# Layer 0's first norm: GpSimd adds pairs of squared tiles, and four products with ones sum them in place of eight

## The chip, the cores and the metric

The kernel runs on one NeuronCore of one Trainium2 chip. A time is device microseconds (us) of one execution; lower is better. The engines are TensorE (PE; PEld is its weight load), VectorE (DVE), ScalarE (ACT), GpSimd (POOL) and SyncE (SP, which issues the DMAs). Each takes its own instructions in the order of the program, and they meet through semaphores only.

## What is computed

A decoder trunk of two layers, on 512 tokens of width 1024. Each layer takes an RMS norm, one input projection whose columns go to four token mixers (differential attention, a short gated convolution, a diagonal state-space model "S5", and Mamba-2), an output projection and a residual; then a second norm and a gated feed-forward part. The change touches only the first norm of layer 0:

```python
def rmsnorm(x, g):
    xf = x.astype(jnp.float32)
    y = xf * lax.rsqrt(jnp.mean(xf * xf, axis=-1, keepdims=True) + EPS)
    return (y * g.astype(jnp.float32)).astype(x.dtype)
...
    for l in range(DEPTH):
        h = rmsnorm(x, ln1_g[l])
        proj = h @ w_in[l]
```

## The kernel before

The activations lie transposed: `x` is 8 tiles (`KD`) of 128 channels by 512 tokens. All large products run as "units": one unit makes 128 output rows from 8 tiles. To keep float32 accuracy out of a faster matmul type, each operand is split in a high part and a low part (`xh` and `xl`, `wh` and `wl`), and a unit is three passes of 8 matmuls: `xl`·`wh` (L504), `xh`·`wh` (L506 or L509) and `xh`·`wl` (L517). For each unit SP loads `raw`, ACT copies it to `wh` (L903), and POOL forms `wl = raw - wh` (L362); buffers are double, so the load of a unit waits for the `wl` of the unit two before it, and the order on POOL (`low()` calls between other work for S5) is written out by hand.

The gain is folded into `xh` and `xl`, so the units of a norm can start before the norm's root is known; the factor `rbc` (one per token, the same in all partitions) multiplies the results as DVE takes them out of PSUM (`scaled`, L1201). In layer 0, for each tile `k`: ACT makes `xh` (L912) and the square of the tile in `G[:, k % 2]` (L918); DVE makes `xl` (L1187, inputs `x` and `xh` in SBUF); TensorE runs `first_square(k)`, a float32 product of a 128x128 block of ones with the square (L530), summing over the channels in bank 7, and then the two products of unit 0 with tile `k`. ACT's square of tile `k` waits for the product of tile `k - 2`, since `G` has two places for it. When the eighth is summed, ACT forms `rbc` (L924, L926).

Between the `xl` tiles DVE also runs the first steps of the S5 tables (`s5_phases`, L1329 to L1342), one step after each tile, then `s5_decay` (L1346 to L1354) and `s5_values` (L1361 to L1381), which waits for sines that ACT computes from the phases. Only then it takes out units 0 and 1 (L1201, tile `z`). POOL, after the `wl` of units 0, 1 and 2, waits for that first `z` (`unit_out`) before its S5 work begins (`power_terms`, L398), and the `wl` of unit 3 stands behind it.

Of the kernel before, what the change touches and what calls it, by code (L numbers as in the profile page):

```python
# [10 lines left out]
ALU = mybir.AluOpType  # L11
ACT = mybir.ActivationFunctionType
# [4 lines left out]
KD = D // P  # L17
# [55 lines left out]
def build(nc, A):  # L73
    with ExitStack() as ctx:
        arena_end = [0]

        def sb(name, shape, dt=F32, at=None):

            size = int(np.prod(shape[1:])) * (2 if dt == BF16 else 4)
            size = -(-size // 32) * 32  # L80
            off = arena_end[0] if at is None else at
            if at is None:
                arena_end[0] += size
            offsets[name] = off
            return nc.alloc_sbuf_tensor_at(name, list(shape), dt, offset=base + off)

        def sem(name):
            return ctx.enter_context(nc.semaphore(name))
# [6 lines left out]
        x = sb("x", [P, KD, T])  # L95
        xh = sb("xh", [P, KD, T], F32R)
        xl = sb("xl", [P, KD, T], F32R)
# [14 lines left out]
        G = sb("G", [P, 6, T])  # L112
# [21 lines left out]
        def early(name, shape, dt=F32):  # L134
            t = sb(name, shape, dt, at=pre_end[0])
            pre_end[0] += -(-int(np.prod(shape[1:])) * 4 // 32) * 32
            return t
# [6 lines left out]
        ones0 = early("ones_first", [P, P])  # L144
        phases = []
        for l in range(L):
# [35 lines left out]
        bank = [ctx.enter_context(nc.psum_tensor(f"bank{b}", [P, T], F32)) for b in range(8)]  # L182
# [9 lines left out]
        act_bank = [sem(f"act_bank{b}") for b in range(8)]  # L192
        dve_free = [sem(f"dve_free{b}") for b in range(8)]
        act_free = [sem(f"act_free{b}") for b in range(8)]
        unit_done, unit_out, resid = sem("unit_done"), sem("unit_out"), sem("resid")
# [3 lines left out]

        x_loaded = [sem(f"x_loaded{k}") for k in range(KD)]  # L200
        rates_loaded, lam_go, lam_exp, mask_ready = [sem(n) for n in ("rates_loaded", "lam_go", "lam_exp", "mask_ready")]
        ones_ready, sq_summed = sem("ones_ready"), sem("sq_summed")
        pre_loaded, par_loaded, cst_loaded, late_loaded = [
            sem(n) for n in ("pre_loaded", "par_loaded", "cst_loaded", "late_loaded")]
        mats_full, out_done = sem("mats_full"), sem("out_done")
# [5 lines left out]
        xh_full, sq_full, sq_free, xk_ready, rms_ready = [  # L211
            sem(n) for n in ("xh_full", "sq_full", "sq_free", "xk_ready", "rms_ready")]
# [31 lines left out]
        def counter():  # L244

            at = {}

            def nth(s, k=1):
                at[s.num] = at.get(s.num, 0) + k
                return at[s.num]  # L250
            return nth
# [16 lines left out]
        def par_of(l, name, i=0, n=1):  # L268
            return par_all[:, l, PARAMS[name][0] + i:PARAMS[name][0] + i + n]
# [79 lines left out]
        def _(pool):  # L349
            nth = counter()  # L350
            own, owned = chain(pool_own)
            tt = nc.gpsimd.tensor_tensor
            unit = iter(range(len(UNITS)))
            temp_free = []

            def low():
                g = next(unit)
                p, cols = g % 2, COLS[g]
                pool.wait_ge(wh_full, g + 1)
                if g >= 2:  # L360
                    pool.wait_ge(unit_done, g - 1)
                tt(wl[:, p, 0:cols], raw[:, p, 0:cols], wh[:, p, 0:cols].bitcast(F32),  # L362
                   ALU.subtract).then_inc(wl_full, 1)
# [75 lines left out]

            nc.gpsimd.memset(ones0[:, :], 1.0)  # L440
            nc.gpsimd.memset(eps_all[:, :], EPS).then_inc(ones_ready, 1)
            for l in range(L):
                low()
                for s in range(NIN - 1):
                    low()
                    if s == 1:
                        power_terms(l, 0)
                        nc.gpsimd.memset(kernels[:, :, :, :], 0.0)
                    if 2 <= s <= 4:
                        for n in ((1, 2), (3,), (4, 5))[s - 2]:  # L450
                            power_terms(l, n)
                    if s == 5:
                        pool.wait_ge(late_loaded, 32)
                        output_matrix(l)
                    if 6 <= s <= 8:
                        state_terms(l, s - 6)
                    if 9 <= s <= 10:
                        table(l, 0, s - 9)
                    if 11 <= s <= 12:
                        for n in ((3, 4), (5,))[s - 11]:  # L460
                            state_terms(l, n)
                    if 13 <= s <= 14:
                        table(l, 1, s - 13)
                    if 17 <= s <= 24 and s - 17 != WHOLE_MEAN:
                        pool.wait_ge(sqk_ready, 8 * l + s - 16)
                        tt(sq_low[:, :], G[:, 2, :], sq_high[:, :].bitcast(F32), ALU.subtract).then_inc(sqk_low, 1)
                    if s in (15, 21):
                        s5_imaginary(l, (s - 15) // 6)
                for _ in range(16 + 2 * (2 * FHALF + 8)):
                    low()  # L470
# [3 lines left out]
        def _(pe):  # L474
            mm = nc.tensor.matmul
            nth = counter()
# [4 lines left out]
            def claim(b, freed, k=1):  # L481

                if b in free_at:
                    pe.wait_ge(*free_at[b])
                if freed is xbc_silu:
                    raised(unit_out)
                free_at[b] = (freed, raised(freed, k))

            def unit(b, K, hi, lo, out, ready=None, within=None, each=None):

                g = next(number)
                p = g % 2
                assert b % 2 == p
                pe.wait_ge(wh_full, g + 1)
                claim(b, out)

                parts = [range(K)] if ready is None else [range(K - 1), [K - 1]]
                for part, ks in enumerate(parts):
                    for k in ks:
                        if ready is not None:  # L500
                            if each is not None:
                                each(k)
                            pe.wait_ge(ready, nth(ready))
                        mm(bank[b][:, :], wh[:, p, k * P:(k + 1) * P], lo[:, k, :], start=(k == 0), stop=False)  # L504
                        if ready is not None:
                            w = mm(bank[b][:, :], wh[:, p, k * P:(k + 1) * P], hi[:, k, :], start=False, stop=False)  # L506
                    if ready is None:
                        for k in ks:
                            w = mm(bank[b][:, :], wh[:, p, k * P:(k + 1) * P], hi[:, k, :], start=False, stop=False)  # L509
                    if ks[-1] == K - 1:  # L510
                        w.then_inc(wh_free, 1)
                    if within is not None:
                        within()
                    if part == 0:
                        pe.wait_ge(wl_full, g + 1)
                    for k in ks:
                        w = mm(bank[b][:, :], wl[:, p, k * P:(k + 1) * P], hi[:, k, :], start=False, stop=(k == K - 1))  # L517
                w.then_inc(unit_done, 1)
# [2 lines left out]
                for i in range(n):  # L521
                    unit(i % 2, K, hi, lo, out, ready if i == 0 else None)

            def first_square(k):

                if k == 0:
                    pe.wait_ge(ones_ready, 1)
                    claim(7, act_free[7])
                pe.wait_ge(sq_full, nth(sq_full))
                w = mm(bank[7][:, :], ones0[:, :], G[:, k % 2, :], start=(k == 0), stop=(k == KD - 1))  # L530
                w.then_inc(*((sq_summed, 1) if k < KD - 1 else (act_bank[7], 1)))

            def rms_sum():

# [241 lines left out]
            early_hi, early_lo = mh[:, MIXB:MIXED, :], ml[:, MIXB:MIXED, :]  # L776
            for l in range(L):
                if l == 0:
                    unit(0, KD, xh, xl, unit_out, xk_ready, each=first_square)
                else:  # L780
                    unit(0, KD, xh, xl, unit_out, xk_ready)
                    rms_sum()
# [103 lines left out]
        def _(act):  # L886
            fn = nc.scalar.activation
            nth = counter()
            unit = iter(range(len(UNITS)))
# [15 lines left out]
            def norm_tile(l, k, gain, arrived=None):  # L905

                n, p = next(normed), k % 2
                if arrived is None:
                    act.wait_ge(resid, nth(resid))
                else:  # L910
                    act.wait_ge(arrived[k], 16)
                fn(xh[:, k, :], x[:, k, :], ACT.Copy, scale=par_of(l, gain, k)).then_inc(xh_full, 1)  # L912
                if arrived is None:
                    if n - 1 > KD:
                        act.wait_ge(sq_free, n - 1 - KD)
                elif k >= 2:
                    act.wait_ge(sq_summed, k - 1)
                fn(G[:, p, :], x[:, k, :], ACT.Square).then_inc(sq_full, 1)  # L918

            logged = counter()  # L920

# [35 lines left out]
            for l in range(L):  # L957
# [143 lines left out]
                for n in range(STEPS):  # L1101
# [5 lines left out]
                    w = (n % NQ + 1) * P  # L1107
# [780 lines left out]
```

## Time and profile before

| | us |
|---|---|
| median of 3 timed runs | 1314.2 |
| lowest, highest | 1313.98, 1315.82 |
| span of the profiled execution | 1310.8 |
| PE busy in the span | 1290.9 |
| DVE busy | 849.4 |
| POOL busy | 637.2 |
| ACT busy | 493.5 |

The span goes from the first to the last instruction of the profiled execution. The page gives no time of that execution from outside; against the median of the timed runs the span is 3.4 us short, which is what lies around it. The granted clock of TensorE is 1.000 over the span. Busy time of PE is not time at its peak, since matmuls are pipelined and their ends are modelled.

### The profile page before, as it was taken

The page shows a single profiled execution, that of the slowest core. Times are in us where ns is not written, and L with a number is a line of the kernel's source. Part 1 is how long each engine was busy: PE and PEld are TensorE (multiplying, and loading weights), DVE is VectorE, ACT ScalarE, POOL GpSimd, SP SyncE. Part 2 cuts the span into 40 slices and gives each one's busy share as a digit, 9 for nine tenths or more (in the row PEclk, how much of TensorE's full clock was granted, in tenths as well). Part 3 has the DMA queues.
Part 4 walks back from the last instruction along what each step waited for, and adds up shares of the span by engine and source line. Part 5 has one row for each costly group of instructions (what it writes and reads, how often), then busy time and mean ns, then how long its engine had stood idle before and what let it go on. Part 6 is the DMA issues. An engine that isn't in the chain of part 4 may idle for free.

```text
span 1310.8 us, 15989 instructions
## 1 busy us (share of the span) xinstructions
PE 1290.9 (98%) x6218; PEld 1054.8 (80%) x6218; DVE 849.4 (65%) x1142; ACT 493.5 (38%) x758; POOL 637.2 (49%) x302
## 2 busy tenths in 40 slices
PE   7999999999999999999999999999999999999999
PEld 4888886787888888888878888867878888888887
DVE  8789885846888117775237799677477761377720
ACT  6332556744223112223344245566432221122220
POOL 2986661144444444444468776512444444444442
PEclk9999999999999999999999999999999999999999
DMA  6232331123333323333232322301333233233332
GB/s 222 81 97 65 97 89 33 28 94 113 97 97 115 101 74 97 97 98 110 84 111 82 87 65 92 87 25 53 99 106 97 97 106 103 81 97 97 109 111 87
DMA packets 40939, 120.49 MB, mean 92 GB/s; under 512 B 6432, under 2 KB 10656, under 8 KB 40864
## 3 DMA queue, kind: packets, MB, share of 16 engines
q1 hardware_dynamic: 40864, 119.46, 29.3%
q8 instruction: 50, 0.82, 0.3%
q14 instruction: 25, 0.20, 0.0%
HBM read 114.20 MB, written 2.10 MB: 89 GB/s over the span
## 4 chain that ended last, share of the span: by engine, by line
PE 90%; DVE 5%; ACT 2%; POOL 2%; DMA 1%; issue 1%; SPq 0%; POOLq 0%; ACTq 0%
PE bank L504 26%; PE bank L517 26%; PE bank L509 25%; PE bank L718 3%; PE bank L506 1%; ACT G L1079 1%; PE bank L766 1%; DMA raw<-in_w_in 1%; POOL wl L362 1%; PE bank L663 1%; PE bank L755 1%; DVE G L1568 1%; PE bank L596 1%; PE bank L611 1%; DVE ssum L1196 1%; PE bank L745 1%
## 5 line engine op out<-in xcount | busy, mean ns | idle before, releaser
L362 POOL TENSOR_TENSOR wl<-raw,wh 128x1024 fp32r<-128x1024 f32 (+3 forms) x208 | 507.1, 2439 | 629.4 <-ACT wh L903 385.1
L903 ACT ACTIVATE wh<-raw 128x1024 fp32r<-128x1024 f32 (+3 forms) x208 | 218.6, 1052 | 267.3 <-PE bank L509 207.9
L504 PE MATMUL bank<-xl,wh 128*128 128x512 f32 x1088 | 282.4, 397 | 0.0
L517 PE MATMUL bank<-xh,wl 128*128 128x512 f32 x1088 | 271.1, 391 | 0.0
L509 PE MATMUL bank<-xh,wh 128*128 128x512 f32 x1056 | 261.0, 389 | 0.0
L504 PEld LDWEIGHTS bank<-xl,wh 128*128 128x128 f32 x1088 | 202.8, 188 | 48.2 <-issue 5.9
L517 PEld LDWEIGHTS bank<-xh,wl 128*128 128x128 f32 x1088 | 203.2, 188 | 41.7
L509 PEld LDWEIGHTS bank<-xh,wh 128*128 128x128 f32 x1056 | 198.3, 188 | 41.5
L1230 DVE TENSOR_TENSOR x<-x,bank 128x512 f32<-128x512 f32 x64 | 43.9, 685 | 228.5 <-PE bank L517 228.4
L504 PE MATMUL bank<-ml,wh 128*128 128x512 f32 x512 | 137.5, 395 | 0.0
L517 PE MATMUL bank<-mh,wl 128*128 128x512 f32 x512 | 127.5, 389 | 0.0
L509 PE MATMUL bank<-mh,wh 128*128 128x512 f32 x456 | 112.9, 389 | 0.0
L517 PEld LDWEIGHTS bank<-mh,wl 128*128 128x128 f32 x512 | 96.1, 188 | 20.0
L504 PEld LDWEIGHTS bank<-ml,wh 128*128 128x128 f32 x512 | 95.3, 188 | 20.8 <-issue 1.4
L1145 ACT ACTIVATE G<-G 128x512 f32<-128x512 f32 x44 | 27.8, 632 | 208.9 <-DVE G L1213 208.9
L1589 DVE TENSOR_TENSOR G<-G 128x512 f32<-128x512 f32 x44 | 101.1, 2298 | 4.6
L509 PEld LDWEIGHTS bank<-mh,wh 128*128 128x128 f32 x456 | 85.6, 188 | 18.0
L1208 DVE TENSOR_SCALAR G<-pad,par_all 128x512 f32<-128x512 f32 x48 | 89.9, 1873 | 1.5
L1201 DVE TENSOR_TENSOR G<-bank,rbc 128x512 f32<-128x512 f32 x68 | 46.7, 687 | 53.7 <-PE bank L517 53.7
L1201 DVE TENSOR_TENSOR pad<-bank,rbc 128x512 f32<-128x512 f32 x60 | 41.4, 689 | 49.6 <-PE bank L517 43.4
L1591 DVE TENSOR_TENSOR ml<-G,mh 128x512 fp32r<-128x512 f32 x44 | 50.1, 1139 | 31.5 <-ACT mh L1148 31.5
L1148 ACT ACTIVATE mh<-G 128x512 fp32r<-128x512 f32 x44 | 27.7, 630 | 106.2 <-DVE G L1589 106.2
(304 smaller groups left out, 1357.8 us busy)
## 6 DMA issues: line engine op xcount, KB each, us to landing
raw<-in_w_gu SPq DMA_DIRECT2D x88, 512.0 KB, 3.5
raw<-in_w_in SPq DMA_DIRECT2D x52, 512.0 KB, 3.7
raw<-in_w_dn SPq DMA_DIRECT2D x32, 704.0 KB, 4.1
raw<-in_w_ol SPq DMA_DIRECT2D x16, 384.0 KB, 3.1
raw<-in_w_oe SPq DMA_DIRECT2D x16, 256.0 KB, 2.6
x<-in_x SPq DMA_DIRECT2D x8, 256.0 KB, 6.2
raw<-in_w_first SPq DMA_DIRECT2D x4, 512.0 KB, 3.8
out_x<-x SPq DMA_DIRECT2D x8, 256.0 KB, 4.6
```

What stands on the lines that cost most here:

```text
L362: tt(wl[:, p, 0:cols], raw[:, p, 0:cols], wh[:, p, 0:cols].bitcast(F32), ALU.subtract).then_inc(wl_full, 1)
L504: mm(bank[b][:, :], wh[:, p, k * P:(k + 1) * P], lo[:, k, :], start=(k == 0), stop=False)
L509: w = mm(bank[b][:, :], wh[:, p, k * P:(k + 1) * P], hi[:, k, :], start=False, stop=False)
L517: w = mm(bank[b][:, :], wl[:, p, k * P:(k + 1) * P], hi[:, k, :], start=False, stop=(k == K - 1))
L718: w = mm(bank[V_BANK[t]][:, :], x_part[:, 2 * j + k, t * P:(t + 1) * P], w_part[:, p, k * T:(k + 1) * T], start=(j == part == k == 0), sto ...
L903: fn(wh[:, p, 0:cols], raw[:, p, 0:cols], ACT.Copy).then_inc(wh_full, 1)
L1145: fn(G[:, 1, :], G[:, 0, :], ACT.Silu).then_inc(g_silu, 1)
L1201: tt(out, bank[b][:, :].rearrange(order, **sizes), rbc[:, :].rearrange(order, **sizes), MUL).then_inc(unit_out, 1)
L1208: after(ts(out, pad[:, p, 4:4 + T], weights[n - 1], None, MUL))
L1230: tt(x[:, o, :], x[:, o, :], bank[p][:, :], ADD).then_inc(resid, 1)
L1589: tt(G[:, 3, :], G[:, 1, :], G[:, 2, :], MUL).then_inc(h_ready, 1)
L1591: tt(ml[:, i, :], G[:, 3, :], mh[:, i, :].bitcast(F32), SUB).then_inc(hid_ready, 1)
```

## The change

`G` is used in four places instead of two. GpSimd gets four additions (`square_pair`), each of two neighbouring squares in place, after the `wl` of unit 0 and before the `wl` of unit 1; each waits for two squares. TensorE multiplies ones with the four sums (`first_squares`) instead of with the eight squares: ahead of tiles 3, 5 and 7 of unit 0, and after unit 0. ACT's squares of the first four tiles wait for nothing; later ones wait for the product that read their place (tiles 4 and 5 for the first, 6 and 7 for the second).

```diff
@@ gpsimd
+            def square_pair(i):
+
+                pool.wait_ge(sq_full, 2 * i + 2)
+                p = 2 * (i % 2)
+                tt(G[:, p, :], G[:, p, :], G[:, p + 1, :], ALU.add).then_inc(sq_paired, 1)
+
             for l in range(L):
                 low()
                 for s in range(NIN - 1):
+                    if l == s == 0:
+                        for i in range(KD // 2):
+                            square_pair(i)
                     low()
@@ tensor
-            def first_square(k):
-
-                if k == 0:
+            def first_squares(i):
+
+                if i == 0:
                     pe.wait_ge(ones_ready, 1)
                     claim(7, act_free[7])
-                pe.wait_ge(sq_full, nth(sq_full))
-                w = mm(bank[7][:, :], ones0[:, :], G[:, k % 2, :], start=(k == 0), stop=(k == KD - 1))
-                w.then_inc(*((sq_summed, 1) if k < KD - 1 else (act_bank[7], 1)))
+                nth(sq_full, 2)
+                pe.wait_ge(sq_paired, i + 1)
+                w = mm(bank[7][:, :], ones0[:, :], G[:, 2 * (i % 2), :], start=(i == 0), stop=(i == KD // 2 - 1))
+                w.then_inc(*((sq_summed, 1) if i < KD // 2 - 1 else (act_bank[7], 1)))
+
+            def beside_first(k):
+
+                if k >= 3 and k % 2:
+                    first_squares((k - 3) // 2)
...
-                    unit(0, KD, xh, xl, unit_out, xk_ready, each=first_square)
+                    unit(0, KD, xh, xl, unit_out, xk_ready, each=beside_first)
+                    first_squares(KD // 2 - 1)
@@ scalar
-                elif k >= 2:
-                    act.wait_ge(sq_summed, k - 1)
-                fn(G[:, p, :], x[:, k, :], ACT.Square).then_inc(sq_full, 1)
+                elif k >= 4:
+                    act.wait_ge(sq_summed, k // 2 - 1)
+                fn(G[:, p if arrived is None else k % 4, :], x[:, k, :], ACT.Square).then_inc(sq_full, 1)
```

TensorE's first instructions of the program, unit 0 with the products of ones between, stood so before (L530 is the product with ones):

```order
1 L530 MATMUL bank<-G,ones_first 128x512 [waits sq_full,ones_ready,wh_full]
2 L504 MATMUL bank<-xl,wh 128x512 [waits xk_ready]
3 L506 MATMUL bank<-xh,wh 128x512
4 L530 MATMUL bank<-G,ones_first 128x512 [waits sq_full]
5 L504 MATMUL bank<-xl,wh 128x512 [waits xk_ready]
6 L506 MATMUL bank<-xh,wh 128x512
7 L530 MATMUL bank<-G,ones_first 128x512 [waits sq_full]
8 L504 MATMUL bank<-xl,wh 128x512 [waits xk_ready]
9 L506 MATMUL bank<-xh,wh 128x512
```

In the changed kernel the same place reads as follows (L513 is L504 of before, L515 is L506, and L540 is the product with ones):

```order
1 L513 MATMUL bank<-xl,wh 128x512 [waits xk_ready,wh_full]
2 L515 MATMUL bank<-xh,wh 128x512
3 L513 MATMUL bank<-xl,wh 128x512 [waits xk_ready]
4 L515 MATMUL bank<-xh,wh 128x512
5 L513 MATMUL bank<-xl,wh 128x512 [waits xk_ready]
6 L515 MATMUL bank<-xh,wh 128x512
7 L540 MATMUL bank<-G,ones_first 128x512 [waits sq_paired,ones_ready]
8 L513 MATMUL bank<-xl,wh 128x512 [waits xk_ready]
9 L515 MATMUL bank<-xh,wh 128x512
10 L513 MATMUL bank<-xl,wh 128x512 [waits xk_ready]
11 L515 MATMUL bank<-xh,wh 128x512
12 L540 MATMUL bank<-G,ones_first 128x512 [waits sq_paired]
```

The first product with ones now stands behind the unit's products with tiles 0, 1 and 2, so it runs after `xl` of tile 2.

GpSimd's queue from its first `wl` on was this before:

```order
9 L362 TENSOR_TENSOR wl<-raw,wh 128x1024 [waits wh_full] x2
10 L362 TENSOR_TENSOR wl<-raw,wh 128x1024 [waits unit_done,wh_full]
11 L398 TENSOR_TENSOR s_powered<-bmat,powers 128x1024 [waits mats_full,unit_out]
12 L448 MEMSET s_kernels 128x448 [waits pool_own]
13 L362 TENSOR_TENSOR wl<-raw,wh 128x1024 [waits unit_done,wh_full]
```

And it is this in the changed kernel:

```order
9 L362 TENSOR_TENSOR wl<-raw,wh 128x1024 [waits wh_full]
10 L446 TENSOR_TENSOR G<-G 128x512 [waits sq_full] x4
11 L362 TENSOR_TENSOR wl<-raw,wh 128x1024 [waits wh_full]
12 L362 TENSOR_TENSOR wl<-raw,wh 128x1024 [waits unit_done,wh_full]
13 L398 TENSOR_TENSOR s_powered<-bmat,powers 128x1024 [waits mats_full,unit_out]
```

The four additions (L446) have come between the `wl` of unit 0 and that of unit 1. DVE's order is the same in both.

## Rows read from the trace of the kernel before

**Rows 1.** The page: span, busy time of the engines, chain by engine.
```profile
span 1310.8 us, 15989 instructions
...
PE 1290.9 (98%) x6218; PEld 1054.8 (80%) x6218; DVE 849.4 (65%) x1142; ACT 493.5 (38%) x758; POOL 637.2 (49%) x302
...
PE 90%; DVE 5%; ACT 2%; POOL 2%; DMA 1%; issue 1%; SPq 0%; POOLq 0%; ACTq 0%
```

**Rows 2.** Chain of waits, 0 to 110 us: start, us, what.
```profile
16.76 0.75 DVE xl L1187
...
18.61 2.66 DVE phase L1341
...
25.75 2.75 DVE phase_low L1361
...
31.29 0.61 DVE z L1201
...
31.97 1.93 POOL s_powered L398
...
36.80 3.54 DMA raw<-in_w_in
...
54.90 4.98 DMA raw<-in_w_in
...
83.24 0.34 DVE xbt L1472
...
83.63 1.16 PE bank L663 x8
```

**Rows 3.** Timeline of PE near 83 us: start, us, what, idle before and its end.
```profile
82.03 0.27 PE L563 MATMUL bank<-cst,s_powered 128*128 128x128 f32 x1
83.63 1.16 PE L663 MATMUL bank<-cst,s 128*128 128x128 f32 x8 [1.32 <-DVE xbt L1472]
```

**Rows 4.** Chain of waits, 7 to 35 us: the products of unit 0.
```profile
7.44 2.07 PE bank L530 x2
9.52 0.43 PE bank L504
9.95 0.43 PE bank L506
10.37 1.09 PE bank L530 x2
11.46 0.23 PE bank L504
...
13.26 0.86 PE bank L530 x2
```

**Rows 5.** Timeline of POOL: start, us, what, idle before.
```profile
7.47 2.35 POOL L362 TENSOR_TENSOR wl<-raw,wh 128x1024 fp32r<-128x1024 f32 x1 [6.50 <-ACT wh L903]
18.46 2.38 POOL L362 TENSOR_TENSOR wl<-raw,wh 128x1024 fp32r<-128x1024 f32 x1 [8.64 <-ACT wh L903]
25.68 2.39 POOL L362 TENSOR_TENSOR wl<-raw,wh 128x1024 fp32r<-128x1024 f32 x1 [4.84 <-ACT wh L903]
...
77.40 1.27 POOL L379 TENSOR_TENSOR s5f<-s5f,s5h 128x512 f32<-128x512 f32 x1
...
109.35 1.53 POOL L379 TENSOR_TENSOR ssum<-ssum,s5h 128x512 f32<-128x512 f32 x1
```

**Rows 6.** Timeline of DVE: start, us, what, idle before.
```profile
9.09 1.28 DVE L1187 SCALAR_TENSOR_TENSOR xl<-x,par_all,xh 128x512 fp32r<-128x512 f32 x1 [2.41 <-ACT xh L912]
10.29 0.55 DVE L1329 TENSOR_TENSOR phase<-thh,rates 128x384 f32<-128x384 f32 x1
...
15.43 0.75 DVE L1187 SCALAR_TENSOR_TENSOR xl<-x,par_all,xh 128x512 fp32r<-128x512 f32 x1 [0.30 <-ACT xh L912]
...
109.77 1.66 DVE L1212 SCALAR_TENSOR_TENSOR G<-pad,par_all,G 128x512 f32<-128x512 f32 x1
111.47 0.75 DVE L1213 SCALAR_TENSOR_TENSOR G<-pad,par_all,G 128x512 f32<-128x512 f32 x1
```

**Rows 7.** Timeline of ACT: start, us, what, idle before.
```profile
12.83 0.63 ACT L918 ACTIVATE G<-x 128x512 f32<-128x512 f32 x1
...
17.35 1.04 ACT L903 ACTIVATE wh<-raw 128x1024 fp32r<-128x1024 f32 x1
```

**Rows 8.** Busy time in windows: length, then PE, PEld, DVE, ACT, POOL, PEclk, DMA.
```profile
9.10:31.20 22.10, 22.10 (x89) 14.16 (x88) 20.52 (x57) 15.61 (x23) 5.49 (x3) 1.00 0.64 232
32.00:85.00 53.00, 51.68 (x259) 43.00 (x258) 41.22 (x76) 20.26 (x30) 51.92 (x31) 1.00 0.28 87
```

More of the change, by code:

```diff
@@ L201, in build @@
         rates_loaded, lam_go, lam_exp, mask_ready = [sem(n) for n in ("rates_loaded", "lam_go", "lam_exp", "mask_ready")]
-        ones_ready, sq_summed = sem("ones_ready"), sem("sq_summed")
+        ones_ready, sq_paired, sq_summed = sem("ones_ready"), sem("sq_paired"), sem("sq_summed")
         pre_loaded, par_loaded, cst_loaded, late_loaded = [
```

## The prediction

> **What bounds the kernel now.** I read the page first, then the chain of waits around the change, then the timelines of the engines on it. The page [rows 1] says that PE is busy 1290.9 of 1310.8 us and holds 90% of the chain. Over the whole program that is true, and it suggests that four matmuls less are four matmuls gained. The change, however, lies in the first 25 us, so that stretch must be read by itself. There the chain of waits [rows 2] runs through PE only until tile 6; then it goes over to DVE (`xl` of the last tile at 16.76, the phase steps, the tables) as far as the first `z` at 31.29, from there to POOL (`s_powered` at 31.97), and on through POOL, loads of weights that POOL's `wl` releases (36.80, 54.90) and DVE, until the transposed Mamba tile `xbt` at 83.24. PE comes back to the chain at 83.63, and there it had been waiting: 1.32 us idle, ended by DVE [rows 3]. So up to 83.63 us PE has 1.32 us to spare, and what sets the program's end is when DVE gets to `z`. From 83.63 on the chain is tied link by link, so a shift of that point is a shift of the end.
>
> **What is removed.** Eight products with ones become four. One takes 0.86 us at the full clock in unit 0, against 0.23 us for a product of the unit; the first ones were slower, the products of tile 0 taking 0.43 us [rows 4]. Four of them are 4 x 0.86 = 3.44 us of PE. ACT also loses its short waits for them. On the path this is worth little: PE's earlier arrival at 83.63 would only lengthen the 1.32 us that it waits there. Before 16 us PE did pace ACT and so DVE, but DVE filled the time between the `xl` tiles with its phase steps; the one stop of DVE between tile 1 and `z` that the removal could give back is the 0.30 us ahead of `xl` of tile 6 [rows 6]. I count the removal as a gain of 0 to 0.3 us.
>
> **What is added.** Four additions of 128x512 on POOL. The same form (`L379`, both inputs in SBUF, written in place) takes 1.27 us alone and 1.53 us when DVE was in its way [rows 5]. POOL had 8.64 us idle between its first two `wl` [rows 5], so POOL itself can hold them: 4 x 1.27 = 5.1 us. The price lies with DVE. In the trace a DVE instruction that reads two operands from SBUF stands still while POOL works: L1341, 0.55 us like other phase steps of 128x384 [rows 6], took 2.66 us at 18.61 [rows 2] because the `wl` that began at 18.46 ran until 20.84 [rows 5]; L1361 took 2.75 us in the same way at 25.75 [rows 2], against the `wl` from 25.68 on [rows 5]; and `xl` of tile 1, issued at 9.09 while the first `wl` ran until 9.82, took 1.28 instead of 0.75 us [rows 6]. For an addition of just this kind there is a pair of rows: L1212 was issued at 109.77 behind L379 (109.35 to 110.88) and took 1.66 us, where its twin L1213, with nothing on POOL, took 0.75 [rows 5, 6]. So one addition costs the DVE instruction behind it 1.66 - 0.75 = **0.91 us**.
>
> In the stretch of the additions DVE has nothing but such instructions: `xl` (inputs `x` and `xh`) and the phase steps, and it is busy for 20.52 of the 22.10 us between 9.1 and 31.2 [rows 8]; the rest is the short steps between dependent instructions. Laid out in the order of the queues:
>
> - The first `wl` ends at 9.8; `xl` of tile 1, which waited for it, goes first, then addition 0 (squares 0 and 1 are long there) from about 10.3 to 11.5. Phase step 0, issued at 10.29, stands behind it: +0.9.
> - `xl` of tile 2 then runs near 11.7 instead of 10.8. Squares 2 and 3 are done by then, addition 1 follows and holds phase step 1: another +0.9, and `xl` of tile 3 comes near 13.9.
> - The first product with ones stands on PE behind unit 0's products with tile 2, so it ends between 14.3 (full clock) and 15.2 (half). ACT's square of tile 4, at 12.83 before [rows 7], waits for that, and behind it on ACT wait `xh` of tiles 5 to 7, the last squares and the copy of `wh` of unit 1, which move from 17.35 [rows 7] to about 19.2. DVE loses part of this gap to waiting, but spends most of it on the steps that it was late with.
> - Additions 2 (from about 17.1) and 3 (from about 19.4) hold phase steps 4 and 5: +0.9 and +0.9. Then the `wl` of unit 1 follows directly and holds DVE as it did before, now at `xl` of tile 7 instead of at L1341. The `wl` of unit 2 holds it once more, as before.
>
> The waits for ACT in the third step replace DVE's old 0.30 us and fall in with the backlog. So the sum is 4 x 0.91 = 3.64 us, and 3.6 us is what the layout gives for `z`: near 34.9 instead of 31.29. PE's unit 1 begins at about 24.7, 3.1 us later than before, since the products with tile 7 wait for its `xl`; four products less are more than eaten by that. The load of unit 3's weights, which waits for the `wl` of unit 1, starts some 2 us later as well, but ACT copies it only after unit 2's, so nothing waits for it.
>
> From `z` on everything in the chain keeps its distances: POOL is busy for 51.92 of the 53 us from 32 to 85 [rows 8], so it can make nothing up. **Sum:** span 1310.8 + 3.6 = 1314.4; with the 3.4 us that lie around the span, 1317.8 us, against the median of 1314.2.
>
> **Bounds of the unknown prices.** The trace has no addition inside this stretch. Below: an addition whose block falls into time in which DVE waits for ACT costs nothing. That can hold for the two late ones (2 and 3), as ACT is the one that is late there: 2 x 0.91 = 1.8 us, and up to 0.3 less for the old stop, 1.5. Above: DVE's instruction comes right behind each addition and the additions run at 1.53 us as at 109.35: 4 x 1.53 = 6.1, less the 4 x 0.2 us of its own start-up that a held instruction has behind it (0.75 against the 0.55 that xl of tile 1 took from 9.82 to 10.37): 5.3. I take 0.91 each because that row is the nearest: same form on both engines, and DVE as dense.
>
> The Trainium skill, "SBUF — State Buffer", section "Who interferes with whom", says that a DVE instruction with two SBUF inputs and a GpSimd instruction that reads SBUF share a port pair, which the first one holds for its whole length. That every instruction behind an addition then pays its whole length would be, as an estimate, 4 x 1.27 = 5.1 us; the pair at 109 us shows 0.91, less than the length, so the measured price stands in the sum.
>
> **The rivals.**
>
> *Partly hidden (about as fast).* The late additions land where DVE waits for `xh`, and only two or three blocks count: +0.5 to +2.6 us, 1314.7 to 1316.8. For it: ACT is 1.4 us or more late from tile 4 on. Against it: by then DVE is two blocks behind and has phase steps 2 and 3 to make up. It decides from two hidden blocks on.
>
> *The clock rises late (slower still).* Before, PE worked without a gap from 7.44 on, and its products went from 0.43 to 0.23 us between 9.95 and 11.46 [rows 4], that is from 1.2 to 2.4 GHz. Now it has only 0.86 us of work per tile at first and stands between tiles. If unit 0 stays at the lower level until its last pass, the seven `wl` products, the third and fourth product with ones and tile 7's products take twice as long: of 7 x 0.23 + 2 x 0.86 + 3 x 0.23 = 4.0 us extra, some 2 lie under the wait for `xl` of tile 7, and 2 delay `rbc`, the sines behind it on ACT, and `z`: +5 to +6, 1319.2 to 1320.2. The Trainium skill, "TensorE: Matmul & The Clock Gate", Part 1, has the clock follow how busy the engine has been; whether these gaps are enough, no row here shows.
>
> *The additions do not hold DVE (no change).* Then `z` moves only by what ACT loses or gains, -0.5 to +0.8 us: 1313.7 to 1315.0. Against it stand the four rows above.
>
> *A block goes away (faster).* The two `wl` cost DVE 2.66 - 0.55 = 2.1 and 2.75 - 0.55 = 2.2 us [rows 2]. If the `wl` of unit 1, or that of unit 2, came to lie where DVE waits for ACT anyway, its block would be free. With one of them gone and the additions half hidden the result is about 0; it ends faster only if both go and no more than one addition counts: 0.9 - 4.3 = -3.4, 1310.8 us. Against it: behind phase 8, DVE has no wait for ACT long enough.
>
> **How the numbers follow.** This kernel's runs spread so that a change under 0.2%, 2.6 us, can't be told from none. Chances: four blocks as forecast (+2.7 to +5.3) 0.62; clock late 0.08; partly hidden 0.21; additions that don't hold DVE 0.05; a block goes away 0.04. So slower 0.70, same 0.26, faster 0.04. The range: the upper end, 1319.8, takes the bound of 5.3 and part of the late clock; the lower, 1315.3, cuts the partly hidden case at +1.1.
>
> **What would show it.** Right: four POOL rows of 1.3 to 1.7 us between the first two `wl`; DVE rows of `xl` or phase steps at 1.4 to 1.7 us beside them; the square of tile 4 after 14 us; the first `z` near 35 us; PE still idle, for more than 1.3 us, ahead of L663's rows. Wrong: `z` before 33 us; DVE's rows at their old lengths beside the additions; or the idle time ahead of those rows gone, which would put PE itself on the chain.

## The result and the profile after

The changed kernel took 1319.4 us (median of 5 runs, 1319.16 to 1319.79), the kernel before 1314.34 beside it (5 runs): 5.06 us slower, ratio 1.0035, 95% interval 1.0024 to 1.0045. The forecast was 1317.8 us in a range up to 1319.8, so sign and range held, and the point was 1.6 us too low.

The page of the profile after, the same lines as in [rows 1]:

```profile
span 1317.4 us, 15978 instructions
...
PE 1290.1 (98%) x6210; PEld 1052.9 (80%) x6210; DVE 855.5 (65%) x1142; ACT 493.1 (37%) x758; POOL 643.7 (49%) x306
...
PE 89%; DVE 5%; ACT 2%; POOL 2%; DMA 1%; issue 1%; SPq 0%; POOLq 0%
```

PE is busy for 0.8 us less and the span is 6.6 us longer: work was taken from an engine for which this stretch does not wait. DVE is busy for 6.1 us more with the same 1142 instructions, so some of them stood still. The chain of waits, which answers to [rows 2] and [rows 4] (start, us, what), names the places:

```profile
9.38 2.35 DVE xl L1203
11.73 1.55 DVE phase L1345
13.28 1.68 DVE xl L1203
15.00 0.80 PE bank L513
16.22 1.72 PE bank L540 x2
17.96 0.64 ACT G L934
18.60 0.62 ACT xh L928
19.25 0.75 DVE xl L1203
20.00 1.36 DVE turns L1353
...
37.95 0.61 DVE z L1217
38.63 1.92 POOL s_powered L398
```

Before, the chain came through PE to tile 6 and then to DVE. Now it is DVE's from 9.38 on, with one way round over PE and ACT from 15.00 to 19.25: the product of `xl` of tile 2, the first product with ones, the square of tile 4 that waited for it, `xh` of tile 5, and back to DVE. From `z` on it is the old chain, 6.66 us later.

POOL's timeline, to be held against [rows 5]:

```profile
8.81 2.36 POOL L362 TENSOR_TENSOR wl<-raw,wh 128x1024 fp32r<-128x1024 f32 x1 [7.84 <-ACT wh L919]
11.14 3.25 POOL L446 TENSOR_TENSOR G<-G 128x512 f32<-128x512 f32 x2
19.81 1.33 POOL L446 TENSOR_TENSOR G<-G 128x512 f32<-128x512 f32 x1 [5.41 <-ACT G L934]
22.08 1.56 POOL L446 TENSOR_TENSOR G<-G 128x512 f32<-128x512 f32 x1 [0.94 <-ACT G L934]
23.61 2.81 POOL L362 TENSOR_TENSOR wl<-raw,wh 128x1024 fp32r<-128x1024 f32 x1
```

And DVE's, against [rows 6]:

```profile
11.65 1.62 DVE L1345 TENSOR_TENSOR phase<-thh,rates 128x384 f32<-128x384 f32 x1
13.20 1.74 DVE L1203 SCALAR_TENSOR_TENSOR xl<-x,par_all,xh 128x512 fp32r<-128x512 f32 x1
14.87 0.54 DVE L1347 TENSOR_TENSOR phase_low<-s,rates 128x384 f32<-128x384 f32 x1
...
17.13 0.34 DVE L1351 TENSOR_SCALAR turns<-turns 128x384 f32<-128x384 f32 x1
19.25 0.75 DVE L1203 SCALAR_TENSOR_TENSOR xl<-x,par_all,xh 128x512 fp32r<-128x512 f32 x1 [1.77 <-ACT xh L928]
19.91 1.45 DVE L1353 TENSOR_SCALAR turns<-turns 128x384 f32<-128x384 f32 x1
...
22.41 1.78 DVE L1203 SCALAR_TENSOR_TENSOR xl<-x,par_all,xh 128x512 fp32r<-128x512 f32 x1
24.12 3.31 DVE L1355 SCALAR_TENSOR_TENSOR phase<-turns,phase 128x384 f32<-128x384 f32 x2
...
37.87 1.28 DVE L1217 TENSOR_TENSOR z<-bank,rbc 128x512 f32<-128x512 f32 x2
```

The two queues read like a zip. Addition 0 holds phase step 0 (1.62 us where it took 0.55), addition 1 holds `xl` of tile 2 (1.74 for 0.74), addition 2 holds a phase step (1.45 for 0.35), addition 3 `xl` of tile 7 (1.78 for 0.74), and behind it the `wl` of unit 1 holds the pair at 24.12, as it held L1341 before. The four holds are 1.07 + 1.00 + 1.10 + 1.04 = 4.21 us. The fifth item is the 1.77 us in which DVE stands for ACT at 19.25. Before, it stood 0.30 us ahead of `xl` of tile 6 [rows 6], and a little ahead of `xl` of tiles 5 and 7 too:

```profile
13.69 0.35 DVE L1335 TENSOR_SCALAR turns<-turns 128x384 f32<-128x384 f32 x1
14.11 0.75 DVE L1187 SCALAR_TENSOR_TENSOR xl<-x,par_all,xh 128x512 fp32r<-128x512 f32 x1
14.78 0.35 DVE L1337 TENSOR_SCALAR turns<-turns 128x384 f32<-128x384 f32 x1
...
16.10 0.55 DVE L1339 SCALAR_TENSOR_TENSOR phase<-turns,phase 128x384 f32<-128x384 f32 x1
16.76 0.75 DVE L1187 SCALAR_TENSOR_TENSOR xl<-x,par_all,xh 128x512 fp32r<-128x512 f32 x1
```

From the start of a phase step to the start of the `xl` behind it, these are 0.42, 0.65 and 0.66 us. Where ACT is in time, the same steps take 0.27, 0.27 (with four idle additions, below: 16.62 to 16.89) and 0.47 us (21.94 to 22.41 in this trace). So the old stops cost 0.72 us together. The new one costs 2.12 - 0.27 = 1.85 us (17.13 to 19.25), 1.13 more. ACT's row (against [rows 7]) says for whom ACT was waiting:

```profile
17.96 0.64 ACT L934 ACTIVATE G<-x 128x512 f32<-128x512 f32 x1 [5.22 <-PE bank L540]
```

PE's timeline shows that product at 16.02, the same product two places later, unit 1's first pass, and the wait that answers to [rows 3]:

```profile
16.02 1.91 PE L540 MATMUL bank<-G,ones_first 128*128 128x512 f32 x2
...
18.73 1.02 PE L540 MATMUL bank<-G,ones_first 128*128 128x512 f32 x2
...
26.27 2.39 PE L513 MATMUL bank<-xl,wh 128*128 128x512 f32 x8
...
90.21 1.05 PE L678 MATMUL bank<-cst,s 128*128 128x128 f32 x7 [1.37 <-DVE xbt L1488]
```

The first product took 1.91 us and a later one 1.02, so PE was still at its lower level (1.2 of 2.4 GHz) when it reached the first. This is read from the length of the products. The granted clock of the profile reads 1.00 in that stretch too (the row ends with PEclk, DMA share and GB/s), so that column alone would not show it:

```profile
16.00:17.80 1.80, 1.80 (x4) 0.75 (x3) 1.48 (x4) 0.00 (x0) 0.00 (x0) 1.00 1.06 403
```

PE still waits for DVE at 90.21, by 1.37 us, and that point lies 6.58 us later than before. The shift of `z` is the shift of the end.

Not all of the 6.6 us is the change's. The first weights landed later in this execution: the first `wl` began at 8.81, against 7.47 in the profiled execution of before [rows 5], 1.34 us that the change can't have made. From the start of the first `wl` to the first `z` it was 31.21 - 7.47 = 23.74 us before (31.21 is the row of DVE's timeline that the chain [rows 2] gives as 31.29) and is 37.87 - 8.81 = 29.06 now: 5.3 us more, which fits the 5.06 of the timed runs, and the holds and the stop make up 4.21 + 1.13 = 5.34 of it. This distance, **wl to z** below, is what I compare between kernels. Where two values are given for a difference, they are against the two profiles of the kernel before (23.74 here, 23.56 in its second).

### The profile page after: what moved, and what is told of

Same layout as the page of the kernel before. It is cut to its first block, busy times and chain, and to the rows that moved or that the text cites. A ratio compares the mean times of both kernels' runs of the same rounds, so it can differ in the third digit from the quotient of the medians.

```text
span 1317.4 us, 15978 instructions
## 1 busy us (share of the span) xinstructions
PE 1290.1 (98%) x6210; PEld 1052.9 (80%) x6210; DVE 855.5 (65%) x1142; ACT 493.1 (37%) x758; POOL 643.7 (49%) x306
## 4 chain that ended last, share of the span: by engine, by line
PE 89%; DVE 5%; ACT 2%; POOL 2%; DMA 1%; issue 1%; SPq 0%; POOLq 0%
PE bank L513 26%; PE bank L526 26%; PE bank L518 24%; PE bank L733 3%; PE bank L515 1%; POOL wl L362 1%; ACT G L1095 1%; PE bank L781 1%; DMA raw<-in_w_in 1%; DVE xl L1203 1%; PE bank L678 1%; PE bank L770 1%; DVE G L1584 1%; PE bank L611 1%; PE bank L626 1%; DVE ssum L1212 1%
## 5 line engine op out<-in xcount | busy, mean ns | idle before, releaser
L513 PE MATMUL bank<-xl,wh 128*128 128x512 f32 x1088 | 281.6, 397 | 14.2 <-ACT wh L919 8.8
L513 PEld LDWEIGHTS bank<-xl,wh 128*128 128x128 f32 x1088 | 203.0, 188 | 64.0 <-ACT wh L919 9.3
L513 PE MATMUL bank<-ml,wh 128*128 128x512 f32 x512 | 137.5, 395 | 0.0
L513 PEld LDWEIGHTS bank<-ml,wh 128*128 128x128 f32 x512 | 95.2, 188 | 20.8 <-issue 1.4
```

## The experiments

Theory: the additions hold DVE by GpSimd's reads of SBUF (about 1 us each), and DVE's longer wait for ACT is the rest. Rivals: the new order of the products with ones costs most of it; or any GpSimd work does; or PE's clock does. Each kernel is compared with runs of the kernel before on the same chip.

| kernel | us | before | ratio, 95% interval | wl to z |
|---|---|---|---|---|
| changed kernel | 1319.4 | 1314.34 | 1.0035, 1.0024 to 1.0045 | 29.06 |
| before, again | 1315.09 | 1314.6 | 1.0004, 0.9995 to 1.0013 | 23.56 |
| changed, no additions | 1315.49 | 1314.7 | 1.0005, 0.9997 to 1.0014 | 25.25 |
| before, 4 idle additions | 1317.58 | 1314.7 | 1.0022, 1.0013 to 1.0031 | 27.19 |
| before, 4 idle writes | 1315.26 | 1314.7 | 1.0004, 0.9995 to 1.0013 | 23.93 |
| before, 8 idle additions | 1321.04 | 1314.6 | 1.0051, 1.0039 to 1.0064 | 31.11 |
| changed, 8 places | 1320.73 | 1314.7 | 1.0045, 1.0031 to 1.0059 | 30.94 |
| changed, PE kept busy | 1317.82 | 1314.37 | 1.0023, 1.0014 to 1.0032 | 27.75 |
| before, PE kept busy | 1313.41 | 1314.37 | 0.9991, 0.9982 to 0.9999 | 23.11 |
| before, POOL fed early | 1313.09 | 1314.6 | 0.9991, 0.9982 to 0.9999 | 24.05 |
| the same, 8 places | 1313.16 | 1314.6 | 0.9989, 0.998 to 0.9997 | 22.87 |
| the same, PE kept busy | 1312.3 | 1314.37 | 0.9983, 0.9974 to 0.9992 | 23.00 |
| the same, with the change | 1318.94 | 1314.37 | 1.0035, 1.0022 to 1.0049 | 30.15 |

### The kernel before, once more

No edit.

> The kernel before once more, for a second profile of it. Theory (the profile of before was an early one, as its first weights landed 1.3 us sooner than in the profile of the changed kernel): the span is 1312 to 1313 us, with the first wh ending near 8.7 us and z near 32.5. Rival (the change itself moved the landing of the first weights): the first wh ends at 7.4 us and z at 31.2 again, span 1310.8. Time 1314.3 either way.

1315.09 us against 1314.6. Its profile has the first `wl` at 8.91, not 7.47, and a span of 1312.0: the profiled execution of before was an early one. The execution took 1313.84, so 1.8 us lie around the span. The 3.4 us of the prediction are those 1.8 and an execution some 1.6 us shorter than the median, most of it the early start.

### The change without its additions

```diff
-                tt(G[:, p, :], G[:, p, :], G[:, p + 1, :], ALU.add).then_inc(sq_paired, 1)
+                nc.gpsimd.memset(mark[:, i:i + 1], 0.0).then_inc(sq_paired, 1)
```

Only the even tiles' squares are summed here; half of the norm is left out. All waits, and the four products, are those of the change; GpSimd only writes one element to signal.

> The changed kernel with the four additions left out: GpSimd only signals (a memset of one element each), so the products with ones sum the even tiles alone and the norm misses half of its squares; the order of the queues and ACT's wait stay. Theory (the additions hold DVE at a shared SBUF read path, some 1.05 us each, and ACT's wait for the first product costs another 1.5 us only because DVE has caught up): without the additions the first z comes at +0.3 to +1.0 us of the kernel before, time 1314.6 to 1315.3. Rival (the new order is the cause: the first product stands behind tile 2 and ACT waits for it): still +4 to +5 us, 1318.5 to 1319.5.

0.8 us above before, which the timed runs can't tell from nothing, and 1.5 to 1.7 by wl to z, where the theory had 0.3 to 1.0. DVE's rows have their old lengths; what is left is its stop for ACT:

```profile
17.31 0.75 DVE L1204 SCALAR_TENSOR_TENSOR xl<-x,par_all,xh 128x512 fp32r<-128x512 f32 x1 [1.76 <-ACT xh L929]
```

The stop is as long as in the changed kernel (1.77), so the additions don't make it; the theory had expected less of it without them. Removing four products gains nothing, and the new order alone, with ACT's wait that belongs to it, costs about 1.5 us at `z`. It is not the larger part.

### The kernel before with four idle additions

```diff
+                    if l == s == 0:
+                        for i in range(4):
+                            pool.wait_ge(sq_full, 2 * i + 2)
+                            own(tt(spare[:, i, :], x[:, 2 * i, :], x[:, 2 * i + 1, :], ALU.add))
                     low()
```

The additions write to a buffer that nobody reads; squares, products and waits are those of before.

> The kernel before with four additions of 128x512 on GpSimd at the place and with the waits of the change, from x into a buffer that nobody reads; eight products with ones and ACT's waits stay as before. Theory: DVE is held four times, z later by 3.6 to 4.4 us, time 1318.0 to 1318.8. Rival (order and ACT's wait): 0 to +0.5 us, 1314.3 to 1314.8.

2.9 us slower, a little less than expected; 3.5 to 3.6 by wl to z. DVE's timeline has the same four holds as the change, 1.07, 1.01, 1.08 and 1.10 us:

```profile
11.14 1.62 DVE L1334 TENSOR_TENSOR phase<-thh,rates 128x384 f32<-128x384 f32 x1
...
13.81 1.75 DVE L1192 SCALAR_TENSOR_TENSOR xl<-x,par_all,xh 128x512 fp32r<-128x512 f32 x1
...
16.89 1.82 DVE L1192 SCALAR_TENSOR_TENSOR xl<-x,par_all,xh 128x512 fp32r<-128x512 f32 x1
...
19.57 1.65 DVE L1344 SCALAR_TENSOR_TENSOR phase<-turns,phase 128x384 f32<-128x384 f32 x1
```

They are 4.26 us together. DVE's old stops for ACT (0.72 us) are gone in return, which is why `z` moved by 3.5 to 3.6. With the 1.5 to 1.7 of the run above this makes 5.0 to 5.3, against 5.3 to 5.5 for the whole change: by wl to z the two parts account for it. In timed runs the two sum to 3.7 of 5.06; the intervals are wide enough for either.

### Four idle writes in their place

```diff
+                            own(nc.gpsimd.memset(spare[:, i, :], 0.0))
```

Memsets of 128x1216, at the same places and with the same waits; behind the fourth, GpSimd also waits until they are done.

> The kernel before with four memsets of 128x1216 on GpSimd in the place of the idle additions, about as long (1.27 us each) but reading nothing. Theory (what is shared is the read path): DVE isn't held, z within 0.3 us of before, 1314.2 to 1314.7. Rival (any work on GpSimd holds DVE, or GpSimd's own lateness with the next wl is what counts): +3.5 to +4.5 us, 1318 to 1319.

No difference that can be measured. POOL's first memset and DVE's rows beside it:

```profile
10.64 1.11 POOL L449 MEMSET spare<- 128x1216 f32 x1
```

```profile
11.18 0.54 DVE L1335 TENSOR_TENSOR phase<-thh,rates 128x384 f32<-128x384 f32 x1
11.65 0.74 DVE L1193 SCALAR_TENSOR_TENSOR xl<-x,par_all,xh 128x512 fp32r<-128x512 f32 x1
```

DVE runs at its old lengths beside a GpSimd instruction that only writes. That rules out "any GpSimd work holds DVE". The Trainium skill, "SBUF — State Buffer", section "Who interferes with whom", says the same: a DVE instruction with two SBUF inputs contends with a GpSimd instruction that reads SBUF, not with one that only writes it. The rows of the two runs agree, 1.62 us beside the addition and 0.54 beside the memset.

### Eight idle additions

Behind each of the four additions stands a second one, with the same inputs and a buffer of its own.

> The kernel before with eight idle additions on GpSimd, two at each of the four places. Theory: twice the hold of the four idle additions, z later by 7 to 9 us, 1321.5 to 1323.5. Rival (the hold saturates, since DVE has waits of its own to hide it in): under 6 us, below 1320.5.

6.4 us slower, under what was expected; 7.4 to 7.6 by wl to z, against 3.5 to 3.6 for four. The price grows with the number. POOL and DVE take turns, one held DVE instruction to each addition:

```profile
11.79 1.63 DVE L1336 TENSOR_TENSOR phase<-thh,rates 128x384 f32<-128x384 f32 x1
13.34 1.75 DVE L1194 SCALAR_TENSOR_TENSOR xl<-x,par_all,xh 128x512 fp32r<-128x512 f32 x1
15.01 1.63 DVE L1338 TENSOR_TENSOR phase_low<-s,rates 128x384 f32<-128x384 f32 x1
```

### The change with PE kept busy

```diff
+            def busy(n):
+
+                for _ in range(n):
+                    mm(bank[6][:, 0:P], ones0[:, :], ones0[:, :], start=True, stop=True)
+
+            pe.wait_ge(ones_ready, 1)
+            busy(28)
...
+                if k in (1, 2):
+                    busy(6)
```

Products of ones with ones, whose result nobody reads, fill PE's gaps ahead of unit 0 and ahead of its tiles 1 and 2.

> The changed kernel, with idle products of ones with ones (128x128, into a bank that is free) on PE: 28 ahead of unit 0 and 6 ahead of tiles 1 and 2 each, so that the clock is up when the first product with ones runs. Theory (DVE is held four times, and stops 1.5 us more for ACT because the first product ran at half the clock): the product takes 0.86 instead of 1.72 us, ACT goes on 0.9 us sooner, -0.5 to -0.9 us of the change: 1318.5 to 1318.9. Rival (most of the loss is the clock, by way of late products and a late rbc): -3 us or more, 1316.4 or less.

1317.82 us, between the two expectations: 1.6 us less than the change, and 3.45 above before. PE's first product with ones now takes 1.02 us, and DVE's stop for ACT is 0.42:

```profile
15.41 1.02 PE L540 MATMUL bank<-G,ones_first 128*128 128x512 f32 x2
```

```profile
17.75 0.76 DVE L1213 SCALAR_TENSOR_TENSOR xl<-x,par_all,xh 128x512 fp32r<-128x512 f32 x1 [0.42 <-ACT xh L938]
```

Wl to z falls by 1.31, the stop by 1.35. So the lower clock up to the first product is what made the stop long. The timed runs alone would not show it, as the 28 products also make the kernel before 1 us faster (next run); the row of the stop does. What is left, 4.0 to 4.2 by wl to z, is the four holds (4.24 us in its rows).

### The kernel before with PE kept busy

The 28 products alone.

> The kernel before with the 28 idle products ahead of unit 0. PE's first products then run at the full clock and PE is some 1.6 us ahead in unit 0. Theory (DVE's tables and GpSimd's chain set the end, not PE): 0 to -0.4 us, 1314.2 to 1314.6. Rival (PE sets the end from the start): -1.6 us, 1313.0.

1 us faster, between theory and rival, with an interval that reaches from -2.4 to -0.1 us. DVE's 0.3 us stop ahead of tile 6 is gone, and wl to z is 0.45 shorter than in the second profile of before. So PE's pace before 16 us sets a little of DVE's, as the prediction allowed; where more than 0.45 should come from I can't show.

### The change with a place for each square

ACT waits for no product (additions and products use the new places):

```diff
-                elif k >= 4:
-                    act.wait_ge(sq_summed, k // 2 - 1)
-                fn(G[:, p if arrived is None else k % 4, :], x[:, k, :], ACT.Square).then_inc(sq_full, 1)
+                fn(G[:, p, :] if arrived is None else squares[:, k, :], x[:, k, :], ACT.Square).then_inc(sq_full, 1)
```

> The changed kernel with a place of its own for each of the eight squares, so ACT never waits for a product; the additions stay. Theory: the four holds of DVE stay (4 x 1.05 = 4.2 us), DVE's extra 1.5 us of waiting for ACT goes, z at +3.7 to +4.3 us, time 1318.0 to 1318.7. Rival (ACT's wait is the cause): nearly all is given back, 1314 to 1315.

A miss: 1320.73 us, slower than the change, where 1318.0 to 1318.7 was expected. DVE's stop for ACT went, and something else came. ACT now copies unit 1's `wh` at 16.37, so its `wl` runs at 18.08 and holds `xl` of tile 4; PE, still at the lower level (0.63 us for a product with `xh` that takes 0.39 later), waits 2.73 us for that tile and is late with the last product with ones; `rbc` and the sines behind it on ACT are late, and DVE waits for the sines. DVE's rows:

```profile
18.46 2.82 DVE L1202 SCALAR_TENSOR_TENSOR xl<-x,par_all,xh 128x512 fp32r<-128x512 f32 x1
...
34.10 0.56 DVE L1376 TENSOR_TENSOR phase_low<-turns 128x384 f32<-128x384 f32 x1 [3.72 <-ACT turns L970]
```

and ACT's:

```profile
30.39 0.69 ACT L939 ACTIVATE rbc<-bank,eps 128x512 f32<-128x512 f32 x1 [11.59 <-PE bank L541]
```

That is the route of the rival "the clock rises late". ACT's wait in the changed kernel kept the `wl` of unit 1 behind the `xl` tiles; a wait that is taken away lets the next collision start.

### POOL fed early, and what can be put on it

In the kernel before, POOL's `power_terms` waits for the first `z`, though it needs only `powers`, which DVE has some 0.6 us sooner:

```diff
-                    pool.wait_ge(unit_out, unit_out_of(l, 0))
+                    pool.wait_ge(*((unit_out, unit_out_of(l, 0)) if l else (powers_ready, 1)))
```

The clearing of `s_kernels` (0.47 us) also went to the program's start. This tests that PE isn't the bound up to the wait of [rows 3]: then POOL's gain must come out at the end.

> The kernel before, where GpSimd's S5 work in layer 0 starts when its input (powers) is ready and not after the first z, 0.65 us sooner, and the memset of 0.47 us that stood behind it is done at the program's start. Theory (the chain from DVE's tables through GpSimd to PE's wait near 83 us sets the end one to one): -1.1 us, 1313.2. Rival (PE sets the end): no change, 1314.3.

1.5 us faster than before, and PE's wait shrank from 1.24 us (the second profile of before) to 0.39:

```profile
84.24 1.16 PE L666 MATMUL bank<-cst,s 128*128 128x128 f32 x8 [0.39 <-DVE xbt L1478]
```

So it is as the prediction read it: without touching a product, an earlier POOL makes an earlier end. The same kernel with eight places for the squares (the eight products kept):

> The same as the kernel whose GpSimd is fed early, and besides a place of its own for each square with the eight products kept, so PE no longer paces ACT. Theory: DVE's 0.30 us of waiting ahead of tile 6 goes as well, -1.4 us, 1312.9. Rival (PE's pace sets DVE's): -2.5 us or more, 1311.8 or less.

1313.16 us, the same as without them, though `z` came 1.2 us sooner after the first `wl`: PE no longer waits near 83 us, so at most the 0.39 us above was left to gain, which these runs can't tell from nothing. With the 28 products of ones ahead of unit 0 as well:

> The kernel whose GpSimd is fed early and whose squares have a place each (where PE no longer waited near 83 us), with the 28 idle products ahead of unit 0. Theory (there PE has become the limit, by less than 1 us): -0.5 to -1.2 us of that kernel, 1312.0 to 1312.6. Rival (PE isn't the limit there either): no change, 1313.2.

1312.3 us, as expected, and 2.1 us under the kernel before: of all kernels here the fastest. Its trace doesn't show why: wl to z is no shorter (23.00 against 22.87), and PE waits 0.37 us near 83 us again. The change put on top of it (additions, four products, PE kept busy between the tiles too):

> The change put on that last kernel: four additions and four products, a place for each square, GpSimd fed early, PE kept busy ahead of unit 0 and of tiles 1 and 2. Theory (each addition holds DVE about 1.07 us whatever PE does): 3 to 4.3 us slower than the same kernel with eight products, 1315.2 to 1316.8. Rival (where PE is the limit the four products saved pay): 1 to 3 us faster than it, below 1311.5.

1318.94 us, 6.6 us slower than without the change. The direction was expected, the size (1315.2 to 1316.8 us) missed. The `wl` of unit 1 held `xl` of tile 4 again, as with eight places above; PE waited 2.50 us for it, and the clock then fell. Windows of its PE (length, busy times, then PEclk):

```profile
20.00:22.00 2.00, 0.36 (x2) 0.30 (x2) 2.00 (x3) 0.00 (x0) 1.04 (x1) 1.00 0.07 27
22.00:24.00 2.00, 1.79 (x8) 1.16 (x6) 2.00 (x4) 0.00 (x0) 0.00 (x0) 0.91 0.87 256
24.00:26.00 2.00, 2.00 (x6) 1.61 (x5) 1.85 (x6) 0.00 (x0) 0.00 (x0) 0.50 0.02 6
```

The granted clock fell behind a stretch with 0.36 us of work in 2, and not in it: 1.00, 0.91, then 0.50. The last pass of unit 0 ran at 1.2 GHz, and `rbc` and the sines were late again, for which DVE stood 2.96 us:

```profile
32.71 0.56 DVE L1392 TENSOR_TENSOR phase_low<-turns 128x384 f32<-128x384 f32 x1 [2.96 <-ACT turns L986]
```

The Trainium skill, "TensorE: Matmul & The Clock Gate", Part 1, has the clock follow how busy the engine was; these rows agree. In no kernel here, then, did the additions pay.

## Why the prediction was right, and where its size was off

- **PE is not the bound up to 83 us.** Right: the wait stands (1.37 us for DVE), the point lies 6.58 us later, and so does the end. POOL fed early shows it from the other side.
- **The removal is worth 0 to 0.3 us.** Right that PE's saved time does not reach the end; wrong that ACT loses its waits for the products. Without the additions, the change's order is a loss of 1.5 to 1.7 us (wl to z). The reading behind the 0.3 was short as well: DVE's old stops came to 0.72 us, not to the one of 0.30.
- **Each addition holds one DVE instruction, 4 x 0.91.** The mechanism is shown by four idle additions (the holds alone), eight (the price grows), and the memsets (a write holds nothing). The size was off: 1.00 to 1.10 us each, 4.21 in place of 3.64, so the twin pair at 109 us was 0.14 short per addition.
- **ACT's waits "replace DVE's old 0.30 us and fall in with the backlog".** This is the step that failed. The new stop cost 1.85 us and replaced 0.72: 1.13 us. The layout let `xl` of tile 2 run freely near 11.7 and had addition 1 hold the phase step behind it, so that this hold would lie in the time in which DVE waits for ACT. In the trace addition 1 follows addition 0 at once (3.25 us for both) and holds `xl` of tile 2 itself: it ended at 14.94, or 13.6 counted from the first `wl`'s old start, where the layout had about 12.5. The product with ones behind it took 1.72 us at the lower clock, the upper end of what the layout allowed, and ended at 17.94 (16.6 by the old start), not between 14.3 and 15.2. DVE had three phase steps and two `xl` to do meanwhile, none of them held, and then stood. The stop itself is no effect of the holds: without additions it is as long (1.76 us). It comes with the new order, and with PE kept busy it shrinks to 0.42. That a hold behind `xl` of tile 2 would have filled part of it is worked out from the order of the queue; no run shows it.
- **The sum.** 4.21 + 1.13 = 5.34, against 5.32 by wl to z. Against the second profile of before, whose old stops come to 0.54 us, it is 4.21 + 1.31 = 5.52, against 5.50. The layout had 3.64, so of the 1.7 us that it fell short, 0.57 are the size of the holds and 1.13 the stop. That the timed 5.06 is so near the bound of +5.3 is luck: the additions did take 1.53 us on average, as the bound has it (6.14 in all), but they held DVE for 4.21, and the rest is the stop.
- **The rivals.** Partly hidden: no, all four holds are in full on DVE. Clock late: half true; of the products with ones only the first was slow, the last pass of unit 0 ran at full speed (seven products in 1.78 us), and DVE did not wait for `rbc` or the sines. The additions don't hold DVE, and a block goes away: no; the `wl` of unit 1 held DVE as before, 2.2 us at 24.12 (3.31 for a pair that took 1.15 before).
- **Unit 1 on PE** was forecast 3.1 us later; it began at 26.27 against 21.56, 3.4 us later when the start's 1.34 are taken off.

## What to carry to other kernels

Before work goes to GpSimd because GpSimd is idle, look at what DVE does at that time: if it is dense with instructions that read SBUF, each GpSimd instruction that reads SBUF costs DVE most of its own length (1.0 to 1.1 us for an addition of 1.27 us here), and it matters which DVE instruction it lands on: a `wl` that held `xl` of tile 4 let PE wait 2.5 to 2.7 us, one that held phase steps did not. Matmuls that are taken out of a stretch in which PE waits later anyway are worth nothing, and the gaps that they leave can cost clock. Lay the queues out instruction by instruction. A wait is hidden only by work that stands between its start and its end in the waiting engine's own queue; a hold that comes ahead of it hides nothing.

## What the runs showed of the hardware that was not expected

- An instruction with one tensor operand was held too: the TENSOR_SCALAR of 128x384 at 19.91 took 1.45 us beside an addition, 0.35 alone.
- The two engines take turns: with eight additions, the first six alternate with six DVE instructions, and each of these additions takes 1.58 to 1.73 us instead of 1.28 us, as the last two of the four idle additions did. GpSimd is held by DVE as well as the other way round.
- A single execution's start moves by more than some of the effects here: the first `wl` began between 7.47 and 9.05 us in these profiles, with nothing changed ahead of it in most of them.
- With 28 products of nothing on PE while it waited for its first weights, the kernel before was about 1 us faster (interval 0.1 to 2.4); its rows account for 0.45 of it.
